# Closing stages with four slots, constants reordered, tables rounded first and 48 unread matmuls in the attention stages of a two-layer hybrid kernel

## The chip, the cores and the metric

The kernel runs on one core of a Trainium2 chip. The metric is the device time of one execution in microseconds (us), the median of the runs. The engines are named as in the profile: PE is TensorE's matmul, PEld its weight load, DVE is VectorE, ACT is ScalarE, POOL is GpSimd, SP is SyncE, which here only issues DMAs. TensorE has two clock levels, 1.2 and 2.4 GHz; the profile's "PEclk" gives the granted clock, 0.50 for the lower and 1.00 for the higher one.

## What is computed

Two layers over 1024 latent tokens and 256 context tokens, width 1024. The even layer runs dense grouped-query attention and a bidirectional RWKV-7 scan side by side; the odd layer runs attention in a window of +-128 tokens with a sink logit per head. Each mixer's output is gated, multiplied by an output projection, normalised and added to the stream:

```python
for l in range(DEPTH):
    ...
    if l % 2 == 0:
        yx, yc = _even_mixer(hx, hc, ...)     # _dense_attention and _rwkv_bidir_scan, _rwkv_readout
    else:
        yx, yc = _odd_mixer(hx, hc, ...)      # _window_attention with sink
    x = x + gt_x * _rms(yx, g_post[l])
    if need_ctx:
        ctx = ctx + gt_c * _rms(yc, g_post[l])

def _rwkv_readout(y, r, kmod, v, rk, gn_w, gn_b):
    mean = jnp.mean(yf, axis=-1, keepdims=True)
    var = jnp.mean(jnp.square(yf - mean), axis=-1, keepdims=True)
    yn = ((yf - mean) * lax.rsqrt(var + GN_EPS)).astype(y.dtype) * gn_w + gn_b
    bonus = jnp.sum(r[None] * kmod * rk, axis=-1, keepdims=True) * v[None]
    ...

# even layer: out = concatenate([oa * silu(ga), ob * silu(gb)]) @ w_out
```

## The kernel before

The program is a row of stages with a barrier between them: modulation, the input projection of layer 0 (`in0`), the RWKV streams, the scan, the dense attention (`attention`, name "dense"), the closing of layer 0 (`closing`, "close0" here; the profile writes `close_` for both), the input projection of layer 1, the windowed attention ("window") and the closing of layer 1 ("close1"). Within a stage each engine has its own list of instructions, written out by hand in the order in which it runs them, and they meet through semaphores. An engine works strictly through its list: whatever waits stops all that stands behind it on that engine.

**`attention`** works in units: one tile of 128 queries and one group of four heads. For a unit TensorE multiplies queries with all keys into `score` (`measure`, L1814 in dense, L1805 to L1810 in window), VectorE reduces that to a row maximum (`highest`, L1727); there is one `score` buffer, so the next `measure` waits for that reduction. When a unit's pieces are through, VectorE makes the negated maximum and a diagonal matrix `shift` (`turn`, L1742 to L1746), TensorE spreads it over the partitions (`broadcast`, L1819) and ScalarE writes it into `QM` (`lower`). Then come the steps, one for each tile of keys: TensorE makes the shifted transposed scores in `turned` (L1831, L1836, at the edges of the window with a mask, L1834), ScalarE exponentiates them into `p` (L1695), TensorE multiplies with V into `outs` (`meet`, L1849). VectorE divides at the end of a unit (`finish`, L1763 and L1767) and counts `out_done`. A unit's maxima are found while the steps of earlier units run; before the first unit there is nothing to run beside them. GpSimd fills constant rows of `KL` and V and rounds `ones`, `ident` and the masks to the type of TensorE's operands, and then (`prepare`) loads the stage's output weights in four blocks and splits them into a high and a low half (`w_hi`, L1683; `w_lo`, L1685).

**`closing`** works in tiles of 128 tokens, ten in close0 and eight in close1. For tile i: in close0 only, TensorE sums the bonus products of the heads (`bonus_sums`, L2127, eight small matmuls in the profile's count), VectorE centres and normalises the scan's output (`centre`, `vary`, `readout`, L2046 to L2071), GpSimd multiplies v with the bonus and adds the bias (`bonus_of`, L2020 and L2023). Then TensorE transposes `o` into `tr` (`turn`, L2137), VectorE multiplies it with the gate (`multiply`, L2077), ScalarE rounds it to `hi`, VectorE subtracts to `lo` (`keep_low`, L2083), TensorE multiplies `hi` and `lo` with the weight halves in two halves of columns (`product`, L236, 24 matmuls for each), ScalarE takes squares and root (L1992), VectorE scales (L2094), GpSimd adds the residual and stores (L2029, L2031).

What sets the order in `closing` before:

- All loaded tiles have three slots (`NL = 3`). SyncE's `load(i)` issues gate, scan output, v, bonus and `o` of a tile in one go and waits for `low` of tile i - 3 before it.
- All engines wait for all constants (`loaded`): identity, `sel`, `gw`, `gb`, `gp` and two rows `gt`. The last three are queued behind the first tile's loads.
- TensorE's list in iteration i: `bonus_sums(i+3)`, `product(i, 0)`, `turn(i+1)`, `product(i, 1)`. VectorE's: `vary(i+2)`, `scale(i-1)`, `readout(i+2)`, `multiply(i+1)`, `centre(i+3)`, `keep_low(i+1)`. GpSimd's: `bonus_of(i+3)`, `add(i-1)`.

## Time and profile before

| | us |
|---|---|
| median of three runs | 2861.19 |
| the three runs | 2861.0, 2861.19, 2869.78 |
| the profiled execution | 2890.62 |
| span of the profiled execution | 2888.8 |
| TensorE busy (matmul) | 2221.3 (77%) |
| VectorE busy | 1297.9 (45%) |
| ScalarE busy | 820.1 (28%) |
| GpSimd busy | 694.0 (24%) |

Stages that the change touches, by the first DMA of each in the trace: dense attention from 1401 us, close0 from 1761, the next projection from 2031, windowed attention from 2361, close1 from 2764 to the end. A busy share is a mean over stages with different limits, so a stage is read by itself: which wait ends last in it, and who stands behind that wait. A busy TensorE is not yet a fast one: the granted clock stands beside it.

### The profile page before, as it was taken

How to read it: one execution, taken by the hardware profiler on the slowest of the kernel's cores; microseconds unless marked ns; L12 is line 12 of the kernel's file. 1: busy time of each engine (PE TensorE's matmuls, PEld its weight loads, DVE VectorE, ACT ScalarE, POOL GpSimd, SP SyncE). 2: the span in 40 equal slices, each digit the busy share in tenths (PEclk: the TensorE clock that was granted, in tenths of full speed). 3: DMA queues.
4: the chain of work that ended last, by engine and by line, in shares of the span. 5: the costliest groups of instructions: out<-in, count | busy, mean ns of one | idle time of the engine just before them, and what ended most of it. 6: DMA issues, size and time to landing. Idle time of an engine off the chain costs nothing. (4 is left out here: it accounts for less than half of the span.)

```text
span 2888.8 us, 59301 instructions
## 1 busy us (share of the span) xinstructions
PE 2221.3 (77%) x25966; PEld 1858.1 (64%) x25966; DVE 1297.9 (45%) x1679; ACT 820.1 (28%) x1389; POOL 694.0 (24%) x616
## 2 busy tenths in 40 slices
PE   7589999922336888788589994658399968999978
PEld 1168888811126777777488884546387757888866
DVE  0344455257943544454344344545554513444422
ACT  0121133133523434444133332111333301233311
POOL 0132255111122323323210001123355624000002
PEclk9789999965668999999799886779699985899989
DMA  7622234135243222221411003232443444111143
GB/s 248 208 97 87 95 90 113 64 127 198 91 153 91 79 75 62 79 74 27 113 52 37 23 26 128 90 120 91 151 140 90 119 105 114 44 52 52 41 152 109
DMA packets 223199, 282.33 MB, mean 98 GB/s; under 512 B 59160, under 2 KB 157592, under 8 KB 221912
## 3 DMA queue, kind: packets, MB, share of 16 engines
q1 hardware_dynamic: 196432, 194.31, 22.1%
q0 software_dynamic: 20176, 81.54, 8.5%
q8 instruction: 206, 3.38, 0.5%
q10 hardware_dynamic: 6336, 2.70, 0.3%
q14 instruction: 49, 0.40, 0.0%
HBM read 190.54 MB, written 87.95 MB: 96 GB/s over the span
## 5 line engine op out<-in xcount | busy, mean ns | idle before, releaser
L236 PE MATMUL in_acc<-in_hi,in_whi 128*128 128x512 f32 (+1 forms) x1024 | 391.8, 383 | 20.4 <-DVE in_lo L599 16.8
L236 PE MATMUL in_acc<-in_lo,in_whi 128*128 128x512 f32 (+1 forms) x1024 | 376.0, 367 | 0.0
L236 PE MATMUL in_acc<-in_hi,in_wlo 128*128 128x512 f32 (+1 forms) x1024 | 375.8, 367 | 0.0
L236 PEld LDWEIGHTS in_acc<-in_hi,in_whi 128*128 128x128 f32 x1024 | 196.3, 192 | 59.1 <-issue 27.9
L236 PEld LDWEIGHTS in_acc<-in_lo,in_whi 128*128 128x128 f32 x1024 | 196.4, 192 | 36.9 <-issue 7.2
L236 PEld LDWEIGHTS in_acc<-in_hi,in_wlo 128*128 128x128 f32 x1024 | 195.9, 191 | 31.6
L1727 DVE TENSOR_REDUCE dense_top<-dense_score 128x1 f32<-128x640 f32 (+1 forms) x144 | 112.3, 780 | 190.0 <-PE dense_score L1814 190.0
L1727 DVE TENSOR_REDUCE window_top<-window_score 128x1 f32<-128x640 f32 (+1 forms) x128 | 101.3, 791 | 211.2 <-PE window_score L1810 211.2
L1849 PEld LDWEIGHTS dense_outs<-dense_V,dense_p 128*128 128x128 f32 x1344 | 183.5, 203 | 4.9 <-ACT dense_p L1695 0.4
L1849 PE MATMUL dense_outs<-dense_V,dense_p 128*128 128x65 f32 x1344 | 179.8, 280 | 0.0
L1849 PEld LDWEIGHTS window_outs<-window_V,window_p 128*128 128x128 f32 x1216 | 167.2, 208 | 5.0 <-ACT window_p L1695 0.6
L1849 PE MATMUL window_outs<-window_V,window_p 128*128 128x65 f32 x1216 | 168.8, 286 | 0.2 <-ACT window_p L1695 0.2
L2009 POOL MEMSET close_eps<- 128x1 f32 x2 | 0.2, 104 | 622.3 <-POOLq L127 622.3
L1254 DVE TENSOR_TENSOR scan_X<-scan_X,scan_small 128x512 f32<-128x512 f32 x80 | 55.0, 688 | 189.5 <-PE scan_small L1382 188.6
L1387 PE MATMUL scan_wide<-scan_XT,scan_Y 64*64 64x64 f32 x3200 | 121.8, 224 | 19.5 <-issue 19.3
L1695 ACT ACTIVATE dense_p<-dense_turned 128x512 f32<-128x512 f32 x168 | 96.6, 597 | 119.5 <-PE dense_turned L1836 119.1
L236 PE MATMUL close_acc<-w_hi,close_hi 128*128 128x512 f32 x288 | 123.7, 429 | 5.2 <-DVE close_lo L2083 5.1
L1141 POOL TENSOR_TENSOR scan_off<-scan_LA,scan_lmask 128x512 f32<-128x512 f32 x100 | 123.9, 1274 | 0.0
L1363 PE MATMUL scan_small<-scan_X,scan_off 64*64 64x64 f32 x3200 | 118.4, 225 | 7.0 <-issue 6.7
L1387 PEld LDWEIGHTS scan_wide<-scan_XT,scan_Y 64*64 64x64 f32 x3200 | 106.8, 135 | 23.6 <-issue 23.5
L236 PE MATMUL close_acc<-w_lo,close_hi 128*128 128x512 f32 x288 | 120.3, 418 | 0.0
L236 PE MATMUL close_acc<-w_hi,close_lo 128*128 128x512 f32 x288 | 119.7, 416 | 0.0
(250 smaller groups left out, 5010.8 us busy)
## 6 DMA issues: line engine op xcount, KB each, us to landing
modulation_w<-in_w_mod SPq DMA_DIRECT2D x12, 2048.0 KB, 8.0
streams<-decay_out POOLq DMA_DIRECT2D x8, 2560.0 KB, 7.8
scan_L<-streams SPq DMA_DIRECT2D x80, 256.0 KB, 3.7
in_raw<-in_w_in_even SPq DMA_DIRECT2D x28, 512.0 KB, 3.8
in_raw<-in_w_in_odd SPq DMA_DIRECT2D x20, 512.0 KB, 3.8
close_ga<-gates SPq DMA_DIRECT2D x18, 512.0 KB, 4.1
gates<-in_outs POOLq DMA_DIRECT2D x32, 256.0 KB, 2.3
window_Q<-qst SPq DMA_DIRECT2D x32, 256.0 KB, 3.0
```

Source lines behind the costliest of these rows:

```text
L236: last = pe.matmul(out, a(k), b(k), start=(k == 0 and x == 0), stop=(k == n - 1 and x == 2))
L1141: pool.tensor_tensor(off[s][:, k], triangles, lmask[:, k + 1:k + 2, :].to_broadcast([P, NU, HD]), ALU.mult).then_inc(off_done, 1)
L1254: dve.tensor_tensor(X[s][:], X[s][:], small[s][:], ALU.subtract).then_inc(x_less[s], 1)
L1363: return pe.matmul(small[s][half_of(1 - c), u, :], off[s][half_of(c), k, u, :], X[s][half_of(c), u, :], start=True, stop=True)
L1387: return pe.matmul(wide[s][half_of(1 - c), u, :], Y[s][half_of(1 - c), u, :], XT[j % 3][half_of(1 - c), u, :], start=True, stop=True)
L1695: act.activation(p[:, s % NP_], turned[s % NTURN][:], ACT.Exp, scale=SCALE).then_inc(expd, 1)
L1727: dve.tensor_reduce(top[:, i % NSLOT, x, r:r + 1], score[:, :, 0:width], AXS, ALU.max).then_inc(topped, 1)
L1849: last = pe.matmul(outs[i % 2][:, r * HW:(r + 1) * HW], p[:, s % NP_, r * P:(r + 1) * P], v, start=(k == 0 and r == 0), stop=(k == n - 1 a ...
L2009: pool.memset(eps[:, 0:1], EPS).then_inc(readied, 1)
```

## The change

It has three parts.

1. `closing`. `NL` is 4 for the scan output, v, bonus and `o`; the gates keep three slots (`NG = 3`) and are loaded by a function of their own, `load_gate`, which waits for `low`. `load(i)` now waits for `turned` of tile i - 4. The constants that all engines wait for are the identity and, in close0, `sel`, `gw` and `gb`; `gp` and `gt` have their own semaphore `gains_in`, are queued behind the second tile's loads, and only VectorE waits for them, ahead of the first `scale`. TensorE's list has `bonus_sums(i+3)` behind `turn(i+1)` instead of ahead of `product(i, 0)`.
2. `attention`, GpSimd and SyncE. The tables are rounded first and the constant rows of `KL` and V are filled behind them, with a semaphore `filled` of their own, for which TensorE waits ahead of the first `turn` and the first `meet`. In the windowed stage masks and sinks are third and fourth in SyncE's queue instead of behind the first group's loads. The first load of the output weights waits for `out_done` of the first unit.
3. `attention`, TensorE. As soon as `ones_r` is rounded, 48 matmuls of `ones_r` with itself, 128x512, write into the last `turned` buffer; nobody reads the result, and the first real use of the buffer overwrites it.

```diff
@@ attention
+    WARM = 48
@@ sync
                 sp.dma_start(ident[:], consts[:, C_ID:C_ID + P]).then_inc(loaded, 16)
                 sp.dma_start(ones[:], consts[0:1, C_ALL:C_ALL + P].to_broadcast([P, P])).then_inc(loaded, 16)
+                if window:
+                    sp.dma_start(masks_raw[:], ...).then_inc(loaded, 16)
+                    sp.dma_start(sinks[:], ...).then_inc(loaded, 16)
...
                 load_group(0)
-                if window:
-                    sp.dma_start(masks_raw[:], ...).then_inc(loaded, 16)
-                    sp.dma_start(sinks[:], ...).then_inc(loaded, 16)
@@ gpsimd
-                pool.memset(KL[HD:P]...); pool.memset(KL[HD:HD + 1]...)   # counted by rounded
                 pool.wait_ge(loaded, 16 * NCONST)
                 pool.tensor_copy(ones_r[:], ones[:]).then_inc(rounded, 1)
...
+                pool.memset(KL[HD:P]...); pool.memset(KL[HD:HD + 1]...); pool.memset(V...)   # counted by filled
                 for b in range(D // BLK if prepare else 0):
+                    if b == 0:
+                        pool.wait_ge(out_done, 1)
@@ tensor
-                pe.wait_ge(rounded, 6 if window else 4)
+                pe.wait_ge(rounded, 1)
+                for _ in range(WARM):
+                    pe.matmul(turned[NTURN - 1][:].rearrange("p (r n) -> p r n", r=R), ones_r[:],
+                              ones_r[:, None, :].to_broadcast([P, R, P]), start=True, stop=True)
+                pe.wait_ge(rounded, 3 if window else 1)
@@ closing
-    NL = 3
+    NL, NG = 4, 3
-        NCONST = 4
+        NCONST = 1
@@ sync
                     if i >= NL:
-                        sp.wait_ge(low, i - NL + 1)
-                    sp.dma_start(ga[:, s], ...).then_inc(ga_in[s], 16)
+                        sp.wait_ge(turned, i - NL + 1)
...
+                def load_gate(i):
+                    t, s = tiles[i], i % NG
+                    if i >= NG:
+                        sp.wait_ge(low, i - NG + 1)
+                    sp.dma_start(ga[:, s], ...).then_inc(ga_in[s], 16)
@@ vector
                     if i == 0:
-                        dve.wait_ge(loaded, 16 * NCONST)
+                        dve.wait_ge(gains_in, 48)
@@ tensor
                 for i in range(-4, N):
-                    if rwkv and 0 <= i + 3 < N:
-                        bonus_sums(i + 3)
                     if i >= 0:
                         product(i, 0)
                     if 0 <= i + 1 < N:
                         turn(i + 1)
+                    if rwkv and 0 <= i + 3 < N:
+                        bonus_sums(i + 3)
```

Where it moves instructions, the two lists stand side by side below, word for word. First TensorE in close0, from its first instruction to the transposes of tile 1; L2137 and L2162 are the transposes of tile 1, L2127 and L2152 the bonus sums. Before:

```order
L2127 MATMUL close_bank_b<-close_sel,close_bo 128x8 x12
L2137 MATMUL close_tr<-close_ident,close_o 128x128 x8
L2127 MATMUL close_bank_b<-close_sel,close_bo 128x8 x4
L236 MATMUL close_acc<-w_hi,close_hi 128x512
...
L236 MATMUL close_acc<-w_hi,close_lo 128x512
L2137 MATMUL close_tr<-close_ident,close_o 128x128 x8
L236 MATMUL close_acc<-w_hi,close_hi 128x512
```

and after the change:

```order
L2152 MATMUL close_bank_b<-close_sel,close_bo 128x8 x8
L2162 MATMUL close_tr<-close_ident,close_o 128x128 x8
L2152 MATMUL close_bank_b<-close_sel,close_bo 128x8 x4
L236 MATMUL close_acc<-w_hi,close_hi 128x512
...
L236 MATMUL close_acc<-w_hi,close_lo 128x512
L2162 MATMUL close_tr<-close_ident,close_o 128x128 x8
L2152 MATMUL close_bank_b<-close_sel,close_bo 128x8 x4
L236 MATMUL close_acc<-w_hi,close_hi 128x512
```

The bonus sums of tile 3 stood ahead of the 24 matmuls of the first half product, and stand behind the transposes now.

Next SyncE at the start of close0, before:

```order
L1942 DMA close_ident<-in_consts 128x128
L1944 DMA close_sel<-in_consts 128x32
L1945 DMA close_gw<-in_gn_w_b 128x512
L1946 DMA close_gb<-in_gn_b_b 128x512
L1929 DMA close_ga<-gates 128x8x128
L1932 DMA close_y<-ydir 128x512 x2
L1933 DMA close_v<-vtok 128x512
L1934 DMA close_bo<-bonus 128x4x128
L1935 DMA close_o<-oa 128x512
L1948 DMA close_gp<-in_g_post 128x1024
L1950 DMA close_gt<-mod 128x1024 x2
```

and after:

```order
L1960 DMA close_ident<-in_consts 128x128
L1962 DMA close_sel<-in_consts 128x32
L1944 DMA close_y<-ydir 128x512 x2
L1945 DMA close_v<-vtok 128x512
L1946 DMA close_bo<-bonus 128x4x128
L1947 DMA close_o<-oa 128x512
L1965 DMA close_gw<-in_gn_w_b 128x512
L1966 DMA close_gb<-in_gn_b_b 128x512
L1953 DMA close_ga<-gates 128x8x128
...
L1953 DMA close_ga<-gates 128x8x128
L1970 DMA close_gp<-in_g_post 128x1024
L1972 DMA close_gt<-mod 128x1024 x2
```

The gate has left a tile's group of loads and follows it; `gw` and `gb` come behind the first tile; `gp` and `gt` behind the second.

Last GpSimd at the start of the dense attention, before:

```order
L1664 MEMSET dense_KL 64x2560
L1666 MEMSET dense_KL 1x2560
L1669 CAST dense_ones_r<-dense_ones 128x128
L1676 MEMSET dense_V 128x20
L1681 DMA dense_w_raw<-in_w_out_even 128x8x256
L1683 CAST w_hi<-dense_w_raw 128x8x256
L1685 TENSOR_TENSOR w_lo<-dense_w_raw,w_hi 128x8x256
```

and after:

```order
L1667 CAST dense_ones_r<-dense_ones 128x128
L1674 MEMSET dense_KL 64x2560
L1676 MEMSET dense_KL 1x2560
L1678 MEMSET dense_V 128x20
L1686 DMA dense_w_raw<-in_w_out_even 128x8x256
L1688 CAST w_hi<-dense_w_raw 128x8x256
L1690 TENSOR_TENSOR w_lo<-dense_w_raw,w_hi 128x8x256
```

The rounding of `ones` is first, and the load of the weights (L1681, now L1686) keeps its place in the row but has the new wait.

## Rows read from the trace of the kernel before

**Rows 1.** the page, TensorE's granted clock, tenths, 40 slices of 72 us

```profile
PEclk9789999965668999999799886779699985899989
```

**Rows 2.** waits in close0: who <- what: us in total, times, longest

```profile
PE close_bank_b L2127 <- DMA close_bo<-bonus: 85.2, 9, 20.0
...
SPq L1929 <- DVE close_lo L2083: 154.1, 7, 24.1
```

**Rows 3.** timeline of close0: start us, us, engine, line, operation

```profile
1828.05 0.37 SPq L1929 DMA_DIRECT2D close_ga<-gates  x1
...
1835.31 1.88 PE L2127 MATMUL close_bank_b<-close_sel,close_bo 128*128 128x8 f32 x8 [8.62 <-DMA close_bo<-bonus]
...
1837.04 0.77 PE L236 MATMUL close_acc<-w_hi,close_hi 128*128 128x512 f32 x1
...
1844.18 1.03 PE L2137 MATMUL close_tr<-close_ident,close_o 128*128 128x128 f32 x8
...
1845.26 1.22 DVE L2077 TENSOR_TENSOR close_ga<-close_tr,close_ga 128x1024 f32<-128x1024 f32 x1 [11.11 <-PE close_tr L2137]
...
1849.83 2.31 DVE L2083 TENSOR_TENSOR close_lo<-close_ga,close_hi 128x1024 fp32r<-128x1024 f32 x1
...
1857.56 0.69 DVE L2071 TENSOR_TENSOR close_o<-close_y,close_v 128x512 f32<-128x512 f32 x1
```

**Rows 4.** the chain that ended last: start us, us, what

```profile
2766.31 8.48 DMA close_gt<-mod
...
2789.63 11.15 PE close_acc L236 x48
```

**Rows 5.** timeline of close0, VectorE

```profile
1777.25 1.22 DVE L2046 TENSOR_REDUCE close_mean<-close_y 128x16 f32<-128x1024 f32 x1 [18.68 <-DMA close_gt<-mod]
...
1801.65 2.29 DVE L2083 TENSOR_TENSOR close_lo<-close_ga,close_hi 128x1024 fp32r<-128x1024 f32 x1
...
1821.15 1.22 DVE L2077 TENSOR_TENSOR close_ga<-close_tr,close_ga 128x1024 f32<-128x1024 f32 x1 [10.10 <-PE close_tr L2137]
...
2003.28 1.23 DVE L2077 TENSOR_TENSOR close_ga<-close_tr,close_ga 128x1024 f32<-128x1024 f32 x1 [3.81 <-PE close_tr L2137]
```

**Rows 6.** stretches: busy us by engine (instructions), PEclk, DMA share, GB/s

```profile
1761.00:1771.00 10.00, 0.00 (x0) 0.00 (x0) 0.00 (x0) 0.00 (x0) 0.14 (x2) 0.54 0.76 221
1771.00:1781.00 10.00, 1.87 (x8) 1.78 (x8) 2.62 (x3) 1.21 (x2) 2.37 (x3) 0.50 1.08 366
```

**Rows 7.** the page, DMA issues: KB each, median us to landing

```profile
close_ga<-gates SPq DMA_DIRECT2D x18, 512.0 KB, 4.1
```

**Rows 8.** timeline of the dense attention's start [idle before <-releaser]

```profile
1405.88 0.29 POOL L1669 CAST dense_ones_r<-dense_ones 128x128 fp32r<-128x128 f32 x1 [0.39 <-DMA dense_ones<-in_consts]
...
1409.53 0.87 PE L1814 MATMUL dense_score<-dense_K,dense_Q 128*128 128x320 f32 x2 [13.50 <-DMA dense_QM<-qst]
...
1434.90 0.60 ACT L1695 ACTIVATE dense_p<-dense_turned 128x512 f32<-128x512 f32 x1 [3.72 <-PE dense_turned L1836]
...
1467.03 0.69 PE L1814 MATMUL dense_score<-dense_K,dense_Q 128*128 128x128 f32 x2 [3.93 <-DVE dense_top L1727]
```

**Rows 9.** two tiles, dense: ns min/median/max of one instruction

```profile
L1742 DVE TENSOR_SCALAR dense_top<-dense_top x16: 169/170/3860, 1424.1 to 1736.7; 128x4 f32<-128x4 f32 x16
...
L1746 DVE TENSOR_TENSOR dense_shift<-dense_ident,dense_ntop x20: 691/691/4891, 1428.2 to 1737.1; 128x512 fp32r<-128x512 f32 x20
```

**Rows 10.** stretches of the two attention stages, columns as rows 6

```profile
1465.00:1478.60 13.60, 10.53 (x40) 9.54 (x41) 4.84 (x8) 2.27 (x4) 1.10 (x1) 0.50 0.00 1
...
2396.00:2431.00 35.00, 33.16 (x128) 29.76 (x128) 10.42 (x18) 7.24 (x14) 19.05 (x9) 0.50 0.40 123
...
2438.00:2475.00 37.00, 36.08 (x143) 33.34 (x144) 8.72 (x17) 7.35 (x14) 0.00 (x0) 0.50 0.10 29
2475.00:2761.00 286.00, 262.03 (x1918) 242.59 (x1917) 125.31 (x269) 94.53 (x186) 0.00 (x0) 1.00 0.15 47
```

**Rows 11.** timeline of the windowed attention's start, TensorE

```profile
2377.98 0.44 PE L1805 MATMUL window_score<-window_K,window_Q 128*128 128x128 f32 x1 [23.78 <-POOL window_V L1676]
```

More of the change, by code:

```diff
@@ L1624, in _ @@
                 sp.dma_start(ones[:], consts[0:1, C_ALL:C_ALL + P].to_broadcast([P, P])).then_inc(loaded, 16)
+                if window:
+                    sp.dma_start(masks_raw[:], edge.rearrange("a p n -> p a n")).then_inc(loaded, 16)
+                    sp.dma_start(sinks[:], sink.rearrange("(a n) -> a n", a=1).to_broadcast([P, ngroups * R])
+                                 ).then_inc(loaded, 16)
                 def load(i):
@@ L1640, in _ @@
                 load_group(0)
-                if window:
-                    sp.dma_start(masks_raw[:], edge.rearrange("a p n -> p a n")).then_inc(loaded, 16)
-                    sp.dma_start(sinks[:], sink.rearrange("(a n) -> a n", a=1).to_broadcast([P, ngroups * R])
-                                 ).then_inc(loaded, 16)
                 for i in range(2, min(4, UN)):
@@ L1825, in turn @@
                     if k == 0:
+                        pe.wait_ge(filled, 2)
                         pe.wait_ge(kl_in[g], 16)
@@ L1842, in meet @@
                     if k == 0:
+                        pe.wait_ge(filled, 3)
                         pe.wait_ge(v_in[g], 16)
@@ L1896, in closing @@
             "scaled", "added")
-        ga_in, o_in = (st.sems(*(f"{n}{s}" for s in range(NL))) for n in ("ga_in", "o_in"))
+        gains_in = st.sem("gains_in")
+        ga_in = st.sems(*(f"ga_in{s}" for s in range(NG)))
+        o_in = st.sems(*(f"o_in{s}" for s in range(NL)))
         x_in, stored = (st.sems(f"{n}0", f"{n}1") for n in ("x_in", "stored"))
-        NCONST = 4
+        NCONST = 1
         if rwkv:
             ydir, vtok, bonus, gn_w, gn_b = rwkv
-            NCONST = 7
+            NCONST = 4
             sel = st.sb("sel", [P, PAIRS, 8])
@@ L1944, in _ @@
                     sp.dma_start(sel[:].rearrange("p a b -> p (a b)"), consts[:, C_SEL:C_ALL]).then_inc(loaded, 16)
+                load(0)
+                if rwkv:
                     sp.dma_start(gw[:], gn_w.rearrange("(a n) -> a n", a=1).to_broadcast([P, BW])).then_inc(loaded, 16)
                     sp.dma_start(gb[:], gn_b.rearrange("(a n) -> a n", a=1).to_broadcast([P, BW])).then_inc(loaded, 16)
-                load(0)
-                sp.dma_start(gp[:], g_post[l:l + 1, :].to_broadcast([P, D])).then_inc(loaded, 16)
+                load_gate(0)
+                load(1)
+                load_gate(1)
+                sp.dma_start(gp[:], g_post[l:l + 1, :].to_broadcast([P, D])).then_inc(gains_in, 16)
                 for r in range(2):
-                    sp.dma_start(gt[:, r], mod[l, r:r + 1, 2 * D:3 * D].to_broadcast([P, D])).then_inc(loaded, 16)
-                for i in range(1, NL):
+                    sp.dma_start(gt[:, r], mod[l, r:r + 1, 2 * D:3 * D].to_broadcast([P, D])).then_inc(gains_in, 16)
+                for i in range(2, NL):
                     load(i)
+                load_gate(2)
                 for i in range(2):
@@ L1957, in _ @@
                         load(i + NL)
+                    if i + NG < N:
+                        load_gate(i + NG)
                     if 2 <= i:
```

35 lines of the change are left out of this document (18 added, 17 removed).

## The prediction

> **What bounds the kernel now.** I went by stage, since the change touches four of the program's stages and leaves the rest word for word. The clock line of the page [rows 1] says where TensorE ran at half its clock (5 is 1.2 GHz, 9 or more is 2.4 GHz): the slices of the first closing stage (1761 to about 2027 us, "close0") show 6, 7, 7, 9, and the one at 2383 us, in the windowed attention, 5. The waits of close0 [rows 2] come next. TensorE waits 85.2 us there for the landing of `bo`, the first thing that a new tile needs, and SyncE, which issues that load, stands 154.1 us in its queue until VectorE has written `close_lo`. So nobody is busy: the stage runs a loop of waits. One turn of it, in order of time [rows 3]: `lo` is written, SyncE issues tile 4's loads at 1828.05; they are in at 1835.31, when TensorE does the bonus sums of that tile, which stand ahead of product(i, 0) in its order; the product starts at 1837.04 in the half clock (a 128x512 matmul every 0.427 us; every 0.232 at the full clock, 11.15 us for 48 [rows 4], so the 7.14 us that these 24 take are 8 of the one, 3.4 us, and 16 of the other); the transposes end at 1845.21; VectorE multiplies from 1845.26 and ends `lo` at 1852.14. That is 24.1 us from load to load. From the multiply of tile 1 (1821.15) to that of tile 9 (2003.28) the eight turns take 182.1 us, 22.8 each [rows 5]. The second closing stage ("close1") has no such loop: TensorE is without a gap once it runs, 11.15 us of products a tile [rows 4] and the transposes; only its start waits, for the last constant.
>
> **The change part by part.**
>
> *Close0, the loop.* The loads of tile i+4 now wait for `turned` of tile i, which comes a product and a `lo` earlier and with one more slot, so data is issued some two turns before its bonus sums; and the bonus sums now stand behind turn(i+1). Both edges of the loop are gone. What is late next? On TensorE a turn then holds the bonus sums (1.88 us in the half clock; at the full clock 1.0, halved as the transposes are, between 0.9 and 1.88), two halves of product (24 x 0.232 = 5.57 each) and the transposes (1.03): 13.2 us. The dependency: from the transposes' end 1845.21 to `lo` at 1852.14 is 6.9 us, against 1.0 + 5.6 = 6.6 of cover; then product 5.6, transposes 1.0: 13.6 us. VectorE's own chain in that turn, from the multiply at 1845.26 to the end of the readout at 1858.25, is 13.0 us without a gap [rows 3]. So the turn becomes **13.6 us**, with TensorE, VectorE and the dependency nearly level. Seven turns of that and one without bonus work (11.15 + 1.03 = 12.2): 107.4 us for 182.1. Bounds: 13.0 (VectorE alone), and 17 if the overlap costs VectorE and GpSimd what it can (rival C).
>
> *Close0, the start.* Before, VectorE begins at 1777.25, when the last of seven constants is in; `lo` of tile 0 ends at 1803.94 [rows 5], with hardly a gap between. Bytes queued up to that landing: 3.75 MB; after the change the mark is 1.75 MB (tile 0's four loads and the two group-norm rows). The queue moves 221 GB/s and then 366 [rows 6], so 2.0 MB are 5.5 us (4 to 7). `lo` of tile 0 ends at 1798.4. It is followed at once by product(0, 0), since tile 3's bonus sums no longer stand ahead; product and transposes from cold are 8.2 us (1837.04 to 1845.21) [rows 3]. Multiply of tile 1: 1806.6 instead of 1821.15. Then 107.4 us: 1914.0 instead of 2003.3. What follows is unchanged. **-89 us**, of which 14.5 in the start.
>
> *Close1.* The first transposes wait for `close_gt`, which lands at 2774.79 [rows 4]. Now they wait for the identity and `o`, issued some 0.5 us into the stage at 2764.3; a load of 512 KB lands 4.1 us after issue at the median [rows 7], so 2768.4. The gains (needed first at 2777) are still in time: 3.5 MB at 366 GB/s. **-6 us** (-4 to -6.4); the products behind it are gapless.
>
> *Dense attention, the 48 products.* They need `ones_r`. GpSimd rounds it at 1405.88 when it was waiting for the landing of `ones`, so moving the memsets behind gains nothing here; the products start at 1406.2. At half clock 0.427 us each for about 3.6 us, then 0.232: 8.4 and 39.6 of them, 12.8 us, until 1419.0. The first score product stood at 1409.53 [rows 8] and cannot pass them: +9.5 us. Against it: (a) the 25.4 us from there to the first `p` (1434.90) hold a wait of VectorE behind GpSimd's `w_lo` (3.86 us for a 4-element instruction that takes 0.17 at the median [rows 9]), which goes, since w's loads now wait for the first `out_done`; (b) a score round's 0.87 us of products [rows 8] are half that at the full clock, 0.44 less. How long the full clock lasts is the question: in each round TensorE waits about as long again for VectorE's reduction, and once before a wait of 3.9 us, until 1467.03, was followed by half clock until 1478.6 [rows 8, 10]. I take two or three rounds, 1.1 us. 25.4 - 3.7 - 1.1 = 20.6: first `p` at 1439.6, **+4.7 us**. (All at full clock: +0.8. All 48 at half clock, 20.5 us: +12.)
>
> *Dense, the weight halves later.* GpSimd's four subtractions move behind the first unit. One of them had cost a 4.89-us `shift` (0.69 at the median [rows 9]) and 13.6 us of half clock with it: 4.2 + 13.6 x 0.42 = 9.9 us [rows 10]. (0.42: in the windowed stage 143 matmuls in 37 us at half clock, 1918 in 286 us at full, 3.9 to 6.7 per us.) In their new places each may meet the few instructions with which VectorE shifts a unit, or miss them (two of four met them before); I take half the cost again. **-5 us** (-10 to +10). The Trainium skill (SBUF — State Buffer, section "SBUF: two separate sides") calls the port that VectorE and GpSimd share an exclusive lock held for a whole instruction; the 3.86 and 4.89 us of rows 9 agree, and by it the moved subtractions are no cheaper, only elsewhere.
>
> *Windowed attention.* Masks and sink are now third and fourth in SyncE's queue, so the tables are rounded before the two memsets of `KL`. I put `ones_r` at 2367.8 (the stage begins at 2361, and dense shows a table in 4.9 us after its start, two more DMAs behind it), the 48 end at 2380.6, and the first score product was at 2377.98 [rows 11]: +2.6, less a round or two at full clock: **+2 us**. Then the clock. Before, this stage ran at half clock from 2396 to 2431 and from 2438 to 2475, TensorE 95% busy, and at full clock ever after [rows 10]: whichever clock it has, it tends to keep. The rounds between the 48 products and the steady part leave TensorE waiting for most of the time, so I expect the lead to be lost before it pays: 0 us (-30 to +15).
>
> **Sum**: -89 - 6 + 5 - 5 + 2 + 0 = **-93 us**. The profiled span goes from 2888.8 to 2796. The unprofiled median is 28 us under the profile; I take the same 93 off it: 2861.2 - 93 = **2768 us**. The half-clock stretches of the windowed attention (72 us, worth 30) may not all be in those runs, one reason for width.
>
> **Rivals.**
> *B, the full clock holds* from the 48 products on. For it: in the steady part both stages keep it for hundreds of us. Against: it was lost at the one thin stretch, at 1465. It gives -4 in dense and -30 in windowed: 2734. The Trainium skill (TensorE: Matmul & The Clock Gate, "HAM oscillation") says that long pauses cost the full clock; the rounds' pauses are short, so by that rule this rival is what happens.
> *C, close0 meets another limit at 17 us a turn*: VectorE's chain of 13.0 already holds 2.31 us for `lo`, where the multiply of the same shape takes 1.22 [rows 3], and GpSimd's results may come later in a shorter turn; DMA needs 2.8 MB a tile, 206 GB/s at 13.6, which the rows say is there [rows 6]. 7 x 3.4 = +24: 2792.
> *D, the clock rises late in the 48 products*: +7.5 in each attention: 2783.
> *E, the other side, slower*: the thin rounds drop the clock and the windowed stage keeps the half clock to its end. 286 us would become 497: +211 against -93, so 2979. It decides from 222 us more of half clock on. Against: it left that state by itself after 35 and after 37 us.
> *F, the two edges are not the loop*: only the starts gain, 20 us: 2842. Against: rows 2 and 3 name each step.
>
> **Chances.** Forecast 0.64, B 0.12, C 0.14, D 0.06, E 0.02, F 0.02. The forecast's own range is 2745 to 2788; with B and C it is 2732 to 2800. A difference under 0.3% (8.6 us) can't be told from none: faster 0.97, same 0.01, slower 0.02.
>
> **What would show it.** Close0: multiplies of tiles 2 to 8 every 13.6 us, clock at 2.4 GHz throughout, no wait for `bo`, first VectorE work at 10 us instead of 16 into the stage. Close1: first transposes 5 us into the stage. Dense: 48 products of 12.8 us, first `p` 38.6 us into the stage (33.9 before), no 3.86-us instruction. Windowed: clock by stretches. Wrong if the turns come at 17 or more, if VectorE waits for `v_done`, or if the clock in the score rounds stays at 2.4 GHz.

## The result, and the profile after the change

| | before | after |
|---|---|---|
| median, us | 2865.49 | 2767.29 |
| lowest and highest, us (runs) | 2861.0 to 2871.87 (4) | 2760.78 to 2770.94 (4) |
| ratio of after to before, 95% interval | | 0.9653 [0.9621, 0.9685] |
| the profiled execution, us | 2890.62 | 2770.94 |
| its span, us, and mean granted clock | 2888.8, 0.871 | 2769.2, 0.899 |

The change takes 98 us off (2865.49 - 2767.29), 3.5%. The forecast was 2768, from -93 us.

By stage, in the two profiles, from the stage's first DMA to the next stage's (in1 is the input projection of layer 1; half clock is the time at 1.2 GHz, us):

```
stage            before   after   difference   half clock before / after
dense attention   360.4   349.4      -11.0       91.3 / 49.0
close0 and in1    599.7   512.8      -86.9
window attention  402.8   379.3      -23.5      109.3 / 48.2
close1            124.9   118.3       -6.6
```

The unchanged stages ahead of them took 8.4 us more in the profile of after (dense begins at 1409.4 instead of 1401.0).

The page of after, TensorE's granted clock [rows 1]; a slice is 69 us now:

```profile
PEclk9789999975557999999989999699699998999989
```

close0 is in slices 26 to 28 of the 40 (from 1758.8 to about 1941 us). Its 6, 7, 7, 9 have become 6, 9, 9: at the stage's start the clock is still low, from 1802 us on it is full.

VectorE in close0 [rows 5], the timeline of after (start us, us, engine, line, operation, idle before). L2071 is L2046 of before, L2108 is L2083, L2102 is L2077:

```profile
1769.50 1.22 DVE L2071 TENSOR_REDUCE close_mean<-close_y 128x16 f32<-128x1024 f32 x1 [13.57 <-DMA close_gb<-in_gn_b_b]
...
1793.94 2.28 DVE L2108 TENSOR_TENSOR close_lo<-close_ga,close_hi 128x1024 fp32r<-128x1024 f32 x1
...
1805.57 1.22 DVE L2102 TENSOR_TENSOR close_ga<-close_tr,close_ga 128x1024 f32<-128x1024 f32 x1 [2.22 <-PE close_tr L2162]
...
1819.27 1.22 DVE L2102 TENSOR_TENSOR close_ga<-close_tr,close_ga 128x1024 f32<-128x1024 f32 x1 [0.66 <-PE close_tr L2162]
...
1832.97 1.23 DVE L2102 TENSOR_TENSOR close_ga<-close_tr,close_ga 128x1024 f32<-128x1024 f32 x1 [0.68 <-PE close_tr L2162]
...
1913.80 1.22 DVE L2102 TENSOR_TENSOR close_ga<-close_tr,close_ga 128x1024 f32<-128x1024 f32 x1 [3.79 <-PE close_tr L2162]
```

The multiplies of tiles 1 to 7 come every 13.70 us. In each of these turns VectorE waits 0.66 to 0.68 us for the transposes, where it waited 10.1 to 14.5. Inside one turn, from the timeline of all engines:

```profile
1819.07 0.96 PE L2152 MATMUL close_bank_b<-close_sel,close_bo 128*128 128x8 f32 x8
...
1819.88 0.48 PE L236 MATMUL close_acc<-w_hi,close_hi 128*128 128x512 f32 x1
...
1823.84 2.32 DVE L2108 TENSOR_TENSOR close_lo<-close_ga,close_hi 128x1024 fp32r<-128x1024 f32 x1
...
1826.21 0.50 PE L236 MATMUL close_acc<-w_hi,close_hi 128*128 128x512 f32 x1 [0.50 <-DVE close_lo L2108]
```

The bonus sums (L2152) follow the transposes and wait for nothing. The only thing that TensorE waits for is `lo`, 0.50 us a turn: this is the dependency that the sum named as the next limit.

close1, the chain of waits of after [rows 4] (start us, us, what):

```profile
2651.28 4.26 DMA close_o<-oc
...
2655.69 1.96 PE close_tr L2162 x8
...
2661.36 7.70 PE close_acc L236 x24
```

The first transposes stand 4.8 us into the stage (2650.9) instead of behind `close_gt`.

The start of the dense attention in after [rows 8], timeline:

```profile
1414.96 13.34 PE L1788 MATMUL dense_turned<-dense_ones_r 128*128 128x512 f32 x48 [10.39 <-POOL dense_ones_r L1667]
...
1428.13 0.46 PE L1823 MATMUL dense_score<-dense_K,dense_Q 128*128 128x320 f32 x2
...
1434.02 0.90 PE L1823 MATMUL dense_score<-dense_K,dense_Q 128*128 128x320 f32 x2 [0.92 <-DVE dense_top L1732]
...
1448.38 0.60 ACT L1700 ACTIVATE dense_p<-dense_turned 128x512 f32<-128x512 f32 x1 [3.73 <-PE dense_turned L1846]
```

The 48 products delay the first score product to 18.7 us into the stage (8.5 before). The score rounds run at the full clock (0.46 to 0.57 us for two products) until 1433.3 us; from there they take 0.90 again. The first `p` comes 39.0 us into the stage (33.9 before).

Two tiles of the dense stage in after [rows 9], ns min/median/max:

```profile
L1747 DVE TENSOR_SCALAR dense_top<-dense_top x16: 169/169/172, 1441.3 to 1734.1; 128x4 f32<-128x4 f32 x16
...
L1751 DVE TENSOR_TENSOR dense_shift<-dense_ident,dense_ntop x20: 691/691/693, 1441.7 to 1734.5; 128x512 fp32r<-128x512 f32 x20
```

The long ones (3860 and 4891 ns) are gone; a `dense_ntop` of 1.20 us (0.16 at the median), held beside `w_lo` 73.8 us into the stage, has come in their place.

### The profile page after: what moved, and what is told of

Read it like the earlier page. It is cut to its first block and busy times, and to the rows that moved or that the text cites. A ratio compares the mean times of both kernels' runs of the same rounds, so it can differ in the third digit from the quotient of the medians.

```text
span 2769.2 us, 59591 instructions
## 1 busy us (share of the span) xinstructions
PE 2198.1 (79%) x26062; PEld 1834.7 (66%) x26062; DVE 1288.5 (47%) x1679; ACT 820.5 (30%) x1389; POOL 693.4 (25%) x616
## 5 line engine op out<-in xcount | busy, mean ns | idle before, releaser
L1732 DVE TENSOR_REDUCE window_top<-window_score 128x1 f32<-128x640 f32 (+1 forms) x128 | 101.2, 791 | 201.5 <-PE window_score L1819 201.5
L1860 PEld LDWEIGHTS dense_outs<-dense_V,dense_p 128*128 128x128 f32 x1344 | 176.0, 196 | 4.7 <-ACT dense_p L1700 0.4
L1860 PE MATMUL dense_outs<-dense_V,dense_p 128*128 128x65 f32 x1344 | 173.2, 273 | 0.0
L1860 PE MATMUL window_outs<-window_V,window_p 128*128 128x65 f32 x1216 | 158.9, 275 | 0.2 <-ACT window_p L1700 0.2
L1860 PEld LDWEIGHTS window_outs<-window_V,window_p 128*128 128x128 f32 x1216 | 155.8, 196 | 3.7 <-ACT window_p L1700 0.6
L236 PE MATMUL close_acc<-w_hi,close_hi 128*128 128x512 f32 x288 | 118.0, 410 | 18.2 <-DVE close_lo L2108 18.2
L1132 POOL TENSOR_TENSOR scan_DG<-scan_LB,scan_lmask 128x512 f32<-128x512 f32 x20 | 25.3, 1265 | 378.9 <-ACT scan_LB L1168 378.9
L1363 PEld LDWEIGHTS scan_small<-scan_X,scan_off 64*64 64x64 f32 x3200 | 109.0, 140 | 14.7 <-issue 13.2
```

The lines of the kernel that those rows point to most:

```text
L236: last = pe.matmul(out, a(k), b(k), start=(k == 0 and x == 0), stop=(k == n - 1 and x == 2))
L1132: pool.tensor_tensor(DG[:], LB[:], lmask[:, 0:1, :].to_broadcast([P, NU, HD]), ALU.mult).then_inc(diagonal, 1)
L1363: return pe.matmul(small[s][half_of(1 - c), u, :], off[s][half_of(c), k, u, :], X[s][half_of(c), u, :], start=True, stop=True)
L1732: dve.tensor_reduce(top[:, i % NSLOT, x, r:r + 1], score[:, :, 0:width], AXS, ALU.max).then_inc(topped, 1)
L1860: last = pe.matmul(outs[i % 2][:, r * HW:(r + 1) * HW], p[:, s % NP_, r * P:(r + 1) * P], v, start=(k == 0 and r == 0), stop=(k == n - 1 a ...
```

## The experiments

The theory after the result had three parts: (1) close0 and close1 carry the gain, through the loop lo - load - bonus sums; (2) the 48 products give nothing; (3) the windowed attention's 23 us come from GpSimd splitting the output weights later. A name in brackets is the run's. The ratio is always to the kernel before in runs of the same session. Stage times come from one profile of each kernel.

### One half of the change alone

[close_only]: `attention` as before, `closing` changed. [attn_only]: the reverse.

> Attention as before, closing stages as in the changed kernel. My theory (the closing's loop of waits is nearly all of it, 87 of 98 us measured stage by stage): 0.967 of the kernel before, about -94 us (-87 close0, -7 close1). Rival (the attention part brings what the profile shows there, 11 + 23 us): -94 too, but then the whole change should be 20 to 35 us better than this one. Close0: VectorE's multiplies every 13.7 us, 182 us for the stage against 269.

> Attention as in the changed kernel, closing stages as before. My theory: the 48 products cost about 5 us at dense's start and 2 at the windowed stage's, the later weight halves give back about 5: 0 to -5 us, ratio 0.998 to 1.0. Rival (the profile's -34 us in the two stages are the change's): -20 to -34 us, ratio 0.988 to 0.993. In the profile: first p 39 us after the dense stage's start in both theories.

Measured: closings alone 2784.98 us, ratio 0.9689 [0.9641, 0.9737]; attention alone 2862.81 us, 0.9962 [0.9929, 0.9996]. So the closings carry about 90 of the 98 us and the whole rearrangement of the attention about 11, at the edge of what can be told from none. The two add up to the whole (0.9689 + 0.9962 - 1 = 0.9651). attn_only lies between what was expected (0.998 to 1.0) and its rival (0.988 to 0.993).

### The closings: which edge of the loop

[order_only] keeps the new order of TensorE's list and takes back the slots and the earlier wait. [starts_only] takes back both and keeps only the constants' and gates' new places. [bonus_first] keeps slots and wait and takes back the order.

```diff
@@ order_only
-    NL, NG = 4, 3
+    NL, NG = 3, 3
-                        sp.wait_ge(turned, i - NL + 1)
+                        sp.wait_ge(low, i - NL + 1)
@@ bonus_first
                 for i in range(-4, N):
+                    if rwkv and 0 <= i + 3 < N:
+                        bonus_sums(i + 3)
                     if i >= 0:
                         product(i, 0)
                     if 0 <= i + 1 < N:
                         turn(i + 1)
-                    if rwkv and 0 <= i + 3 < N:
-                        bonus_sums(i + 3)
@@ starts_only: both
```

> The whole change, but loads in the closings keep three slots and wait for low, as before; the bonus sums stay behind the transposes, and the constants stay in the changed order. Theory 1 (either edge of the loop is enough): the loads of tile i+3 are issued when lo of tile i is written, which is where product(i, 0) begins; they land about 7.3 us later, and the bonus sums stand 5.6 + 1.0 = 6.6 us later, so they wait 0.7 us a turn, which a slack of about that size takes up: turns of 13.7 to 14.5 us, close0 and the next projection together 513 to 519 us (512.8 in the changed kernel, 599.7 before). Rival 2 (the fourth slot and the earlier wait are what opened the loop): turns near 20 us or more, 560 us or more.

> The whole change, but with three slots, the wait for low and the bonus sums ahead of the product as before; in the closings only the order of the constants and gates is changed. Theory 1 (the loop is lo, load, bonus sums, product, transposes): 7.3 + 1 to 1.9 + 5.6 + 1.0 + 6.9 = 21.8 to 22.7 us a turn at the full clock and up to 24 at the half clock, VectorE starts about 5 us earlier: close0 and the next projection together 585 to 600 us. Rival 2 (the position of the constants and the gates did most of the work): turns under 16 us, under 540 us.

> The whole change with the bonus sums back ahead of the first half product; four slots and the wait for turned stay. Theory 1 (either edge is enough): the loads of tile i+3 are issued when turn(i - 1) ends, some 13.7 us ahead of the bonus sums, so they are in: turns of 13.7 us (up to 14.7 if the 1 us of bonus sums now lies between lo and the product), close0 and the next projection together 511 to 520 us. Rival 2 (the order of TensorE's list is what opened the loop, the slots alone don't): turns near 20 us or more, 560 us or more.

Two multiplies of each in a row, VectorE's timeline, starts_only first:

```profile
1811.25 1.22 DVE L2102 TENSOR_TENSOR close_ga<-close_tr,close_ga 128x1024 f32<-128x1024 f32 x1 [9.47 <-PE close_tr L2162]
...
1835.15 1.22 DVE L2102 TENSOR_TENSOR close_ga<-close_tr,close_ga 128x1024 f32<-128x1024 f32 x1 [10.91 <-PE close_tr L2162]
```

order_only:

```profile
1818.05 1.22 DVE L2102 TENSOR_TENSOR close_ga<-close_tr,close_ga 128x1024 f32<-128x1024 f32 x1 [0.67 <-PE close_tr L2162]
...
1831.75 1.22 DVE L2102 TENSOR_TENSOR close_ga<-close_tr,close_ga 128x1024 f32<-128x1024 f32 x1 [0.67 <-PE close_tr L2162]
```

bonus_first:

```profile
1804.10 1.22 DVE L2102 TENSOR_TENSOR close_ga<-close_tr,close_ga 128x1024 f32<-128x1024 f32 x1 [0.69 <-PE close_tr L2162]
...
1817.80 1.23 DVE L2102 TENSOR_TENSOR close_ga<-close_tr,close_ga 128x1024 f32<-128x1024 f32 x1 [0.69 <-PE close_tr L2162]
```

Turns of 23.8 us on the mean of the six from tile 1 to tile 7 (26.0 before), 13.70 and 13.70; close0 and in1 together 580.5, 512.7 and 512.8 us (599.7 before, 512.8 after). These three kernels, and no_lo below, ran once each, so only their stages are compared. In starts_only TensorE waited 70.5 us in 9 waits for `bo` again (who <- what: us in total, times, longest):

```profile
PE close_bank_b L2152 <- DMA close_bo<-bonus: 70.5, 9, 13.8
```

In order_only no wait for it is left inside the loop. **Either edge alone opens the loop**; moving eight small matmuls behind the transposes would have been enough, and the fourth slot adds nothing to the time. What it adds is slack: from tile 4 on, `bo` lands 0.0 to 0.7 us ahead of its sums in order_only, and 21 to 24 us ahead in after. The new places of constants and gates alone gave 19 us (599.7 - 580.5): the multiply of tile 1 stands 53.9 us into the stage instead of 59.8, and from there to tile 9's it takes 168.8 us instead of 182.1. That second part was not forecast (585 to 600 us were expected for the two stages). The traces show where it is: the bonus sums of tiles 4 to 9, which start when `bo` lands, begin 6.2 us behind the end of `lo` on the mean instead of 8.5, six times 2.3 us. The gate's 512 KB stood ahead of `bo` in SyncE's queue before and stand behind it now; that this is the reason fits, but no run tests it alone.

### What is next behind a turn of 13.7 us

[no_lo] leaves the products of `lo` and `w_hi` out in both closings, 16 matmuls instead of 24 in each half; that part of the computation is missing, `lo` is still written and waited for.

> The whole change, with the products of lo and w_hi left out in both closings (16 matmuls for each half instead of 24; part of the computation is gone, lo is still written and waited for). It asks what stands next behind the 13.7 us of a turn in close0. TensorE's own share falls to 2 x 3.7 + 1.0 + 1.0 = 9.4 us, the way over lo to 6.9 + 3.7 + 1.0 = 11.6. Theory 1 (TensorE, the way over lo and VectorE are nearly level, VectorE's chain is 13.0 us): turns of 13.0 to 13.2 us, no wait of VectorE for the transposes. Rival 2 (VectorE's 13.0 hold slack, or its instructions get longer beside GpSimd): turns under 12.5 or above 13.7. In close1 a tile falls from 12.0 to 8.3 us or to what GpSimd and VectorE need.

VectorE's timeline, close0:

```profile
1839.52 1.22 DVE L2102 TENSOR_TENSOR close_ga<-close_tr,close_ga 128x1024 f32<-128x1024 f32 x1
...
1853.95 1.22 DVE L2102 TENSOR_TENSOR close_ga<-close_tr,close_ga 128x1024 f32<-128x1024 f32 x1 [1.46 <-PE close_tr L2162]
1866.85 1.22 DVE L2102 TENSOR_TENSOR close_ga<-close_tr,close_ga 128x1024 f32<-128x1024 f32 x1
```

A third of TensorE's products gone, and the turn falls only from 13.70 to 13.39 us on the mean (six turns from 1786.52 to 1866.85). Two of the six are 12.90 us, VectorE's own chain, with no wait for the transposes. In the other four (13.36 to 14.43) VectorE waits 0.38 to 1.46 us for them, and these are the four in which TensorE, idler now, is at half clock for 3.4 to 6.8 us. Turns of 13.0 to 13.2 without such waits were expected, so the clock is a limit that the expectation left out. TensorE, VectorE and the way over `lo` are indeed nearly level, and another step here must shorten all three. In close1, where nothing but TensorE bounds, the same edit took 29 us off (118.3 to 89.3).

### The 48 products, and how many

[no48] has `WARM = 0`, [warm8] `WARM = 8`.

> The whole change without the 48 unread products. My theory: the products are a loss at the start (first score product 9.5 us later, the full clock kept for only about 5 us after them), so this is 5 to 8 us faster than the whole change: ratio to before about 0.963. First p 30 us after the start of dense. Rival (they keep the windowed stage off the long half clock): 15 to 25 us slower than the whole change, ratio 0.971 to 0.975, with half-clock stretches of 60 us or more in the windowed stage.

> The whole change with 8 unread products instead of 48. At the half clock they take 3.4 us and are over before the first keys are in, so they delay nothing. If the price of the 48 is only the 9 to 10 us by which they run past the keys in dense and about 0.5 to 3 us in the windowed stage, and their yield is the shorter rounds, then: first p 30.7 us into the dense stage (as with none), and the time as with none, 2769 (2760 to 2780). If the 48 buy a faster steady part beyond the first rounds (full clock sooner), warm8 shows more half-clock time than the changed kernel in both stages and the time is no lower than 2767 and up to 2780.

Measured: 2768.89 us, 0.9649 [0.9577, 0.9721], and 2767.74 us, 0.9623 [0.9571, 0.9675]; the whole change 0.9653. The first `p` came 30.7 us into the dense stage without products and 29.8 with 8, against 39.0 with 48. So 48, 8 or none make no difference that can be measured; the 5 to 8 us that no48 was to gain did not show. The 48 hold the first unit up by 8 us in dense and by 6 in window (39.8 us instead of 33.5). In dense they get it back: the stage took 349.0 to 364.4 us in the six profiles with them, 49 to 81 us of it at half clock, and 357.8 and 362.8 us without them and with 8, 92 and 100 us of it at half clock.

### Keeping the full clock through the thin rounds

[hold] is the change with `WARM = 8` and, behind each measurement made before the first steps, three unread products in the round in which TensorE otherwise waits for VectorE. [hold2] adds two ahead of each `broadcast` of the dense stage.

```diff
@@ hold
                     for i, q in due(s):
                         score_free(seen)
                         measure(i, q)
+                        for _ in range(HOLD if s < -AHEAD else 0):
+                            pe.matmul(turned[NTURN - 1], ones_r, ones_r)
@@ hold2, on top
                     for i in after_top(s, 2):
+                        for _ in range(2 if s >= 1 and not window else 0):
+                            pe.matmul(turned[(s - 1) % NTURN], ones_r, ones_r)
                         score_free(seen)
                         broadcast(i)
```

> The whole change, with 8 unread products ahead of the first scores instead of 48, and three unread 128x512 products behind every measurement of scores that is made before the first steps (the rounds in which TensorE otherwise waits for VectorE's maximum). Unchanged otherwise. Theory 1 (the full clock is lost in the thin rounds because TensorE waits for about half of each; filled, it stays): after the first rounds no half clock in either attention stage; the 8 products take 3.4 us at the half clock and end before the first keys are in, and the first p comes about 28 us into the dense stage (39.0 in the changed kernel, 30.7 with no unread products at all); the half-clock stretches that the changed kernel still has (47.7 us in each attention stage) go, worth about 10 us each with the 10 us of products saved: 2750. Rival 2 (a half clock of some length costs nothing here, since the rounds hang on VectorE's reductions and not on TensorE): the first p comes at 30 to 32 us, as with no unread products, and the time is that of no unread products, 2769. Rival 3 (the unread products delay the scores behind them, since they are issued ahead of the next measurement and at half clock three take 1.3 us): first p later than 33 us, 2775 or more.

> The kernel with 8 unread products and three behind every early measurement, and in the dense attention also two unread 128x512 products (0.46 us at the full clock) ahead of each spreading of a unit's maximum, where TensorE waits 0.9 us on the mean for VectorE (15.4 us in 17 waits), written into the one of the four turned buffers that no step uses at that point. Theory 1 (the half-clock stretches in the middle of the dense stage start at these short waits at the units' ends and go when they are filled): half clock in the dense stage 20 us or less instead of 54.7, stage 343 to 347 us instead of 351.9, and the time 5 to 10 us below the kernel without them, which had 0.9565 of before. Rival 2 (a stretch of half clock has another cause, or the fillers end after the wait and cost what they give): half clock 40 us or more, stage 350 to 358 us, no difference. Windowed attention as without them: 357 us.

hold: 2743.67 us, 0.9565 [0.951, 0.9619]. The first `p` came 28.4 us into dense and 27.4 into window. The window stage took 357.0 us, with no half clock behind its first 9 us; dense 351.9, still with 54.7 us of it behind its first 11. Its interval overlaps that of warm8 ([0.9571, 0.9675]), from which it differs by the fillers alone, so in time their yield is not yet clear of noise here. TensorE's timeline in hold's dense stage shows what stands ahead of the first long stretch (1457.7 us, 23.9 long):

```profile
1455.32 0.44 PE L1823 MATMUL dense_score<-dense_K,dense_Q 128*128 128x128 f32 x2 [0.52 <-DVE dense_top L1732]
...
1456.28 0.50 PE L1828 MATMUL dense_score<-dense_shift,dense_ones_r 128*128 128x512 f32 x1 [0.52 <-DVE dense_top L1732]
```

Two waits of half a microsecond, at the end of a unit of the context. In the 13 profiles without fillers there, 40 stretches of half clock begin in the steady part of the dense stage: 28 within 6 us behind such a pair (of 52 pairs, four a profile), the other 12 behind an instruction of VectorE's held beside GpSimd (below). Behind the 170 single waits of 0.92 us in the same stages none begins within 17 us. So it is not the longest waits that the fall follows, but those that stand close together: each pair has a third wait of 0.52 us some 3 us behind it. hold2 fills the second wait: 2726.36 us, **0.9521 [0.9469, 0.9572]**, the best of all, and in its profile a dense stage at the full clock from 9.4 us into the stage to its end (stretch: us, busy us and instructions of PE, PEld, DVE, ACT, POOL, then PEclk, DMA share, GB/s):

```profile
1394.90:1712.30 317.40, 300.46 (x2059) 269.70 (x2057) 142.25 (x240) 107.93 (x188) 29.98 (x14) 1.00 0.17 50
```

The dense stage took 327.4 us; in the 13 other kernels it took 349.0 to 372.0. That speaks for theory 1, with a yield larger than expected (343 to 347 us), 24.5 us against hold for 38 unread products; but it is one profile, and no instruction of VectorE's was held in its dense stage either, where hold's had one. In the timed runs hold2 and hold overlap: hold2's window stage, whose code is hold's, was at half clock for 85 us of its 392.2 in the profile. Against the changed kernel (0.9653 [0.9621, 0.9685]) hold2 is clearly faster.

### Where the windowed attention's 23 us are from

[w_early] is the change without the wait of the weights for the first `out_done`; [late_split] is the kernel before with that wait alone.

```diff
                 for b in range(D // BLK if prepare else 0):
-+                  if b == 0:
-+                      pool.wait_ge(out_done, 1)
```

(the two lines taken out in w_early, put in in late_split)

> The whole change, but the output weights are loaded and split from the start, without the wait for the first out_done. My theory (the early subtraction holds VectorE while nothing runs beside it): 4 us later first p in dense unless the split falls between the instructions, and one or two blocks of 4 us with a stretch of half clock: 5 to 10 us slower than the whole change. Rival (the blocks only move): no difference beyond 3 us.

> The kernel before with one edit: the first load of the output weights, and with it GpSimd's splitting, waits for the first unit's out_done, in both attention stages. Theory 1 (the 29 us that the windowed attention lost came from this wait alone: GpSimd no longer meets the few instructions that decide when the first steps start): windowed attention 370 to 380 us (402.8 before; 373.7 to 379.3 in the kernels with the whole change), half clock in it 50 us or less (109.2 before); dense 350 to 364 us, that is no difference that can be told; total 0.988 to 0.993 of before. Rival 2 (the tables, masks and 48 products did it): windowed attention 395 to 403 us, total within 0.3% of before.

w_early: 2788.24 us, 0.9693 [0.9647, 0.974]; a `dense_shift` of 4.89 us is back, dense 372.0 us, window 387.2. late_split: 2863.61 us, 0.9992 [0.9948, 1.0036], window 398.2 us with 101.2 at half clock. **Part 3 of the theory falls**: the wait alone gives nothing. Inside the changed kernel it may still be worth something: w_early's stages are longer in its profile, and its ratio is higher than that of the whole change (0.9653), about as expected, but the two intervals overlap. The windowed stage over all profiles:

```
window stage, us                                    half clock, us
attention as before: before, close_only      402.8, 402.8      109.3, 109.3
late_split                                   398.2             101.2
the changed attention, six kernels           373.7 to 379.3    35.8 to 48.2
no48 / warm8 / w_early                       367.3 / 372.7 / 387.2    43.0 / 51.8 / 62.9
hold / hold2                                 357.0 / 392.2     8.8 / 85.0
```

What no48 shares with the changed kernel and late_split doesn't have is the order of tables and masks: its first score product stands 9.3 us into the stage, late_split's 16.4, and its first `p` at 33.5 against 40.6. That is 7 us. The rest is the clock, which is full from 43 us into the stage in no48 (49 in after) and from 70 in late_split and before: against before, no48 has 66 us less of half clock, at 0.42 us each 28, and 7 + 28 is its whole 35.5 us (402.8 - 367.3). In the changed kernel the 48 products take the 7 us back (first score product at 17.2, first `p` at 39.8 us, 41.0 before), and its 23.5 us are the clock: 61 us less of half clock, 26 at 0.42 each. Of the 61, 34 lie at the stage's start and 27 in the stretch behind VectorE's held instruction (37.5 us in before, 10.2 in after, none in the other five). late_split, at half clock with TensorE all but fully busy:

```profile
2377.00:2406.80 29.80, 28.88 (x116) 26.37 (x115) 7.13 (x13) 7.07 (x14) 5.33 (x3) 0.50 0.18 54
```

Why the clock rises 9 us behind the first `p` in no48 and 29 us behind it in late_split no run here settles; it stays open.

## Why the prediction was right, point by point

**The loop of close0** (13.6 us a turn): 13.70, with the named dependency, 0.50 us of waiting for `lo`, as the limit, and no wait for `bo`. From the multiply of tile 1 to that of tile 9 it forecast 107.4 us; it was 108.2 (1913.80 - 1805.57). Rival C's 17 us did not come: `lo` stayed at 2.32 us, as before. The six turns that the loop sets were 26.0 us before; the 22.8 of the prediction is a mean with the last two, 15.6 and 10.4 us, which the loop doesn't set and which are the same in every kernel but no_lo. Its sum comes out all the same, because the seventh turn was longer than its 13.6 (15.65) and the last shorter than its 12.2 (10.38): that is luck. It also took both edges together and didn't ask whether one would do: each alone gives the whole yield.

**The start of close0** (first work 10 us in, `lo` of tile 0 at 37.0, multiply of tile 1 at 45.2, of tile 9 at 152.6 us into the stage): 10.7, 37.4, 46.8 and 155.0. Of the 1.6 us missing at tile 1's multiply 0.4 were missing at `lo`. The other 1.2 are product and transposes, 9.4 us for the 8.2 taken: the half clock lasted until 1802. In all -86.9 against -89.

**close1** (-6, transposes 5 us in): -6.6, 4.8 us in.

**The 48 products in dense** (first score product +9.5, rounds shorter by 1.1 us, `p` at 38.6 us): +10.2, 1.4 us, 39.0. The 48 took 13.3 us and not 12.8: their half clock lasted 4.7 us, where the prediction took 3.6, a term for which no row stands. Two or three rounds at the full clock were forecast and four came. The Trainium skill (TensorE: Matmul & The Clock Gate, "HAM oscillation"), by which long pauses cost the full clock, gave rival B. The trace disagrees here: between the 48 products and the fall at 1433.3 no wait of TensorE exceeds 1.0 us.

**The weight halves later in dense** (-5, from -10 to +10): with +4.7 of the products the stage was to stay as it was. In one profile it lost 11.0, but over the six profiles with the changed attention it took 349.0 to 364.4 us, mean 355.3, against 360.4 and 352.0 with that of before: no change, as forecast, and the -11.0 was scatter.

**The windowed attention** (+2, and 0 for the clock, from -30 to +15) is the term that was mis-sized: -23.5, and -28 as the mean of six profiles. The wrong step is the 0 for the clock: 61 us less of half clock came, worth 26 by the prediction's own 0.42. The working looked at the 48 products alone as a source of clock, and there it was right: they lost it in the rounds. It left out that the full clock can come earlier behind the thin rounds (49 us into the stage in after and 43 in no48, instead of 70; why is open), and that GpSimd's splitting in its new place can meet VectorE less: the stretch of 37.5 us that began behind a held instruction is one of 10.2 in after and gone in the other five. Its bound of -30 covered it.

**From profile to median**: the profile of before was among its slower executions (2890.62 against 2838.77 to 2907.58 in all its runs), so -119.6 us of span became -98 of median. The timed attention alone gave -11 and not the -35 of the two stages' profiles, so the 109 us of half clock of before's window stage are probably not in every execution, as the prediction warned. By the granted clock of whole executions, before had 669 to 750 us at half clock in that session, 718 on the mean, and 745 in its profile (twice the missing share of the clock, times the span); attn_only had 666 on the mean. Those 52 us would be worth 22 at 0.42 each, and 11 were timed; the rest stays open. -93 lies near -98 because the closings, 95 of it, were sized well (timed alone: -90), and what was missed in the windowed stage shows in full only in the profiles. That 2767.29 lies within 1 us of 2768 is luck: the gain was 5 us larger, and the kernel before 4.3 us slower (2865.49) than the 2861.2 that the forecast started from.

## What to carry to other kernels

- When a stage's engines all wait in turn, write the loop down edge by edge with its times. Cutting one edge was enough here, and the cheapest was the place of a few small instructions in a list.
- Before the next cut, sum the engines' own chains: here 13.0, 13.2 and 13.6 us, so a third of TensorE's products less gave only 0.3 us a turn in close0.
- Unread products paid where they filled waits that were there anyway (57 of hold's in both stages and 38 more in hold2; clear of noise for the two together, against the changed kernel), and not where they stood ahead of work that could have started.

## What the runs showed of the hardware

**A four-element instruction can cost the full clock for 61 us.** In hold2's window stage VectorE's `window_ntop` (four elements in each partition, 0.16 us at the median) was held beside GpSimd's `w_lo`. First VectorE, then GpSimd, then TensorE, each from its engine's timeline:

```profile
2310.38 2.61 DVE L1742 SCALAR_TENSOR_TENSOR window_ntop<-window_top,window_nsinks_up 128x4 fp32r<-128x4 f32 x1
```

```profile
2308.42 4.55 POOL L1690 TENSOR_TENSOR w_lo<-window_w_raw,w_hi 128x2048 fp32r<-128x2048 f32 x1
```

```profile
2314.45 0.50 PE L1828 MATMUL window_score<-window_shift,window_ones_r 128*128 128x512 f32 x1 [1.49 <-DVE window_top L1732]
```

It ends when `w_lo` ends (2312.99 and 2312.97). TensorE waits 1.49 us for it, and two microseconds later its clock falls (columns as above):

```profile
2268.70:2316.50 47.80, 42.64 (x312) 39.55 (x311) 23.35 (x44) 15.73 (x32) 22.97 (x10) 1.00 0.38 121
2316.50:2377.90 61.40, 58.78 (x235) 54.44 (x235) 15.68 (x33) 11.93 (x23) 6.41 (x2) 0.50 0.13 44
2377.90:2616.00 238.10, 217.94 (x1594) 202.31 (x1593) 103.27 (x223) 77.89 (x153) 0.00 (x0) 1.00 0.14 45
```

3.8 matmuls per us at half clock and 6.7 at full: the stretch cost 26 us (61.4 x (1 - 3.8 / 6.7)). In the 14 profiles six stretches of half clock began in the steady part of a window stage (behind its first 50 us), and each follows a VectorE instruction held for 1.2 to 4.5 us during GpSimd's splitting; of the six profiles whose window stage has no such instruction, none has such a stretch. It does not always cost the clock: five others, held for 1.1 to 2.1 us at the full clock (one each in attn_only, w_early, late_split, after and warm8), were followed by no fall within 16 us. One of the longest, in close_only, ns min/median/max:

```profile
L1751 DVE TENSOR_TENSOR window_sd<-window_ntop,window_sinks_up x32: 153/155/4477, 2293.6 to 2651.6; 128x4 f32<-128x4 f32 x32
```

The Trainium skill (SBUF — State Buffer, section "SBUF: two separate sides") has the exclusive lock that VectorE and GpSimd share; the runs agree (2312.99 and 2312.97 above) and add its price one engine further on. A kernel in which GpSimd splits the weights in a stage without such small instructions on the critical path was not tried.

**The full clock goes at short pauses close together, and can stay away from a busy TensorE.** Behind 28 of 52 pairs of waits of 0.52 us the dense stage fell to half clock for 7 to 34 us, and behind none of the four in hold2, where one wait of each pair is filled; behind none of the 170 single waits of 0.92 us did it fall. Behind the thin rounds TensorE was 97% busy for 30 us at half clock (late_split).
